# A transformer step's mixture-of-experts stage: one chunk body, w1/w3 as the moving operand in three fp32r products, chunks in expert order, rows scattered to tokens

## The reference

```python
def _hier_moe(x, w_group, b_group, w_expert, b_expert, w1, w3, w2):
    xt = x.reshape(b * t, d)                                   # 640 x 1024
    g_p, g_idx = lax.top_k(softmax(xt @ w_group + b_group), 1)
    e_sel = ...                                                # the 4 logits of the chosen group
    e_p, e_idx = lax.top_k(softmax(e_sel), 2)
    gate_w = g_p * e_p / sum(e_p)
    combine = sum(one_hot(g_idx * 4 + e_idx, 16) * gate_w[..., None], axis=1)
    hidden = silu(xt @ w1[e]) * (xt @ w3[e])                   # w1, w3: 1024 x 256, for each e
    return sum_e (hidden * combine[:, e]) @ w2[e]              # w2: 256 x 1024

def _block(x, mod, mixer, ln, moe):
    sh1, sc1, g1, sh2, sc2, g2 = jnp.split(mod[:, None, :], 6, axis=-1)
    y, extras = mixer(x * (1.0 + sc1) + sh1)
    x = _layer_norm(DEEPNORM_ALPHA * x + g1 * y, ln[0], ln[1])
    return _layer_norm(DEEPNORM_ALPHA * x + g2 * _hier_moe(x * (1.0 + sc2) + sh2, *moe), ln[2], ln[3])
```

## Time and profile before

| | |
|---|---|
| median of three runs | 1844.82 us |
| the profiled execution, its own time | 1840.76 us |
| its span, first to last instruction | 1839.0 us |
| mean granted TensorE clock | 0.911 |
| TensorE matmul busy | 1471.5 us, 80% of the span |
| TensorE weight load busy | 1123.9 us, 61% |
| VectorE busy | 737.2 us, 40% |
| ScalarE busy | 425.1 us, 23% |
| GpSimd busy | 220.7 us, 12% |
| moved by DMA | 277.62 MB, mean 151 GB/s |

### The profile page before, as it was taken

How to read it: one execution, slowest core, us unless ns; L and a number is a source line. 1 busy time by engine, 2 the same in 40 slices (tenths; PEclk the granted TensorE clock), 3 DMA queues, 4 the chain that set the end, 5 groups by cost and what they waited for, 6 DMA issues and landing times. The chain is left out here.

```text
span 1839.0 us, 22558 instructions
## 1 busy us (share of the span) xinstructions
PE 1471.5 (80%) x8207; PEld 1123.9 (61%) x8208; DVE 737.2 (40%) x1363; ACT 425.1 (23%) x832; POOL 220.7 (12%) x170
## 2 busy tenths in 40 slices
PE   3699999546888997589993199989997857999970
PEld 1577777446565444578882188877874436777760
DVE  0321212076477343211114835439993750111118
ACT  0321212143343111011112312225551111101113
POOL 1100000022000032100003500010000321100016
PEclk9899999769899998699997599999998877999995
DMA  7665555700000901559994032110007126777763
GB/s 256 227 221 199 199 200 193 174 12 15 17 1 2 298 35 61 176 175 357 358 351 157 35 111 75 58 49 1 1 1 231 57 92 233 273 269 250 258 219 143
DMA packets 177697, 277.62 MB, mean 151 GB/s; under 512 B 13400, under 2 KB 111408, under 8 KB 177616
## 3 DMA queue, kind: packets, MB, share of 16 engines
q1 hardware_dynamic: 167232, 239.15, 38.7%
q0 software_dynamic: 9520, 34.24, 5.3%
q10 hardware_dynamic: 864, 3.15, 0.4%
HBM read 246.90 MB, written 34.85 MB: 153 GB/s over the span
## 5 line engine op out<-in xcount | busy, mean ns | idle before, releaser
L485 PE MATMUL psum<-in_parts 128*128 128x460 f32 (+2 forms) x1800 | 400.1, 381 | 23.2 <-PEq L336 23.2
L485 PEld LDWEIGHTS psum<-in_parts 128*128 128x128 f32 x1800 | 337.2, 189 | 101.6 <-issue 53.0
L785 PE MATMUL psum<-layer 128*128 128x512 f32 x400 | 174.2, 595 | 2.7 <-PEq L711 2.7
L1919 PEld LDWEIGHTS psum<-layer 128*128 128x128 f32 x1280 | 145.7, 192 | 15.1 <-issue 7.7
L1919 PE MATMUL psum<-layer 128*128 128x128 f32 x1280 | 146.4, 275 | 6.7 <-DVE layer L2124 6.7
L1919 PEld LDWEIGHTS psum<-layer,arena 128*128 128x128 f32 x1152 | 135.3, 197 | 13.5 <-issue 7.1
L1919 PE MATMUL psum<-layer,arena 128*128 128x128 f32 x1152 | 136.1, 280 | 5.6 <-DVE layer L2124 3.6
L785 PEld LDWEIGHTS psum<-layer 128*128 128x128 f32 x400 | 75.9, 191 | 95.5 <-issue 95.5
L522 DVE TENSOR_TENSOR in_parts<-in,in_parts 128x920 fp32r<-128x920 f32 (+2 forms) x54 | 62.5, 1158 | 167.3 <-ACT in_parts L517 167.3
L2114 DVE TENSOR_TENSOR layer<-psum,layer 128x256 f32<-128x256 f32 x32 | 13.6, 424 | 222.7 <-ACT layer L2084 222.7
L517 ACT CAST in_parts<-in 128x920 fp32r<-128x920 f32 (+2 forms) x54 | 53.7, 994 | 165.1 <-PE psum L485 154.1
(11 more groups left out here) (312 smaller groups left out, 1980.1 us busy)
## 6 DMA issues: line engine op xcount, KB each, us to landing
arena<-in_moe_w SPq DMA_DIRECT2D x48, 1024.0 KB, 9.3
layer<-in_moe_w SPq DMA_DIRECT2D x48, 1024.0 KB, 8.8
in<-in_ada_w SPq DMA_DIRECT2D x40, 1024.0 KB, 5.7
y_rows<-layer SPq DMA_DIRECT2D x64, 256.0 KB, 8.7
in<-in_od_w_in SPq DMA_DIRECT2D x21, 512.0 KB, 3.6
in<-in_ev_w_in SPq DMA_DIRECT2D x21, 460.0 KB, 3.6
start<-in_ada_w SPq DMA_DIRECT2D x8, 1024.0 KB, 16.2
arena<-mod_rows SPq DMA_DIRECT2D x16, 512.0 KB, 8.6
```

Of the source, the lines that this page charges most:

```text
L485: last = T.matmul(bank(g % W_BANKS)[:, 0:cw], a, b[:, kk], start=(k == 0 and m == 0), stop=(k == KD - 1 and m == 2))
L785: last = T.matmul(bank(g % 4), feats[k][:, t * P:(t + 1) * P], wout[:, k, j * BANK:(j + 1) * BANK], start=(k == 0), stop=(k == kt - 1))
L1919: last = T.matmul(dst[:, (2 * f + m) * P:(2 * f + m + 1) * P], weights[m][:, k, f * P:(f + 1) * P], xT[:, k, :], start=(k == 0), stop=(k = ...
```

## The change

- `up` has the operands the other way round. The turned tokens (128 tokens, 128 features) are the stationary operand, and 128 columns of w1 beside 128 of w3 are the moving one, 256 columns. Both are split in two fp32r parts, high and low, and three products are made (x high by w high, x high by w low, x low by w high): 2 halves of the hidden width x 8 feature blocks x 3 = 48 matmuls of 256 columns. The result has tokens on partitions, so the hidden values must be turned (2 transposes and 2 copies) before `down`, which stays.
- ScalarE makes the high parts (a copy to fp32r), VectorE the low parts (a difference): of the weights, 4 pieces of 128x1024 per expert and engine; of the tokens, 2 pieces of 128x512 per chunk and engine. Expert 0's high parts are made in `router`.
- Chunks are numbered in expert order. All use one body; an expert's last chunk also splits the next expert's weights. The second body is gone. The number of chunks is the same.
- Padded rows carry an index out of bounds, and the gather and the store leave them out. What a chunk puts out is scattered by GpSimd to the row of its (choice, token) in `y_rows`, which now has 1280 rows.
- `xg` and `yb` are single buffers. GpSimd's loop per chunk q: wait for the turn of chunk q+1, gather chunk q+2, wait for the copy-out of chunk q, scatter it, wait until it has landed, and release `yb`.
- The weight loads are in rows of 4 KB throughout (w1 and w3 in halves of 512 KB each). SyncE issues w1 and w3 of expert e+2 when expert e's parts are made, and w2 when its last `down` is done. The loads for `combine` come at the end.
- `combine` loads `y_rows` in five plain transfers of 1 MB on SyncE's queue. The zeros and their waits are gone. The router has three VectorE instructions fewer in the middle and four more behind the last product.

The core of the diff:

```diff
-                        sp.dma_start(y_rows[NE * P:, :], zero_row.partition_broadcast(FURTHER * P)
-                                     ).then_inc(further_zero, 16)
...
-                        sp.wait_ge(further_zero, 16)
...
+        def up_high_of(act, b, f, h):
+            return A.copy(part_up(0, f)[:, h * HK:(h + 1) * HK], raw_piece(b, f, h))
+
+        def up_low_of(dve, b, f, h):
+            ks = slice(h * HK, (h + 1) * HK)
+            return V.tensor_tensor(part_up(1, f)[:, ks], raw_piece(b, f, h), whole(part_up(0, f)[:, ks]), ALU.subtract)
...
+                    def refill(p, b):
+                        e = 2 * p + b
...
+                        for h in range(2):
+                            sp.wait_ge(up_low, read[h])          # read = 4 * e + 3 + h
+                            load_up(sp, b, h, ups[h])            # w1, w3 of e + 2
+                        sp.wait_ge(y_s, done)
+                        load_down(sp, b, dn)                     # w2 of e + 2
...
+                    def gather(q):
+                        pool.indirect_dma_start(out=xg, out_offset=None, in_=h2_rows, in_offset=column(from_i, q, 0),
+                                                bounds_check=TOK - 1, oob_is_err=False).then_inc(xg_in, 16)
+
+                    def scatter(q):
+                        pool.wait_ge(y_a, q + 2)
+                        pool.indirect_dma_start(out=y_rows, out_offset=column(to_i, q, 1), in_=yb.rearrange("p j n -> p (j n)"), in_offset=None,
+                                                bounds_check=2 * TOK - 1, oob_is_err=False).then_inc(y_out, 16)
+                        pool.wait_ge(y_out, 16 * q + 16)
+                        pool.nop().then_inc(y_free, 1)
+
+                    gather(0)
+                    last = entry(pool, 2, LAST)
+                    pool.wait_ge(turned, 1)
+                    gather(1)
+                    with pool.Fori(0, last) as q:
+                        pool.wait_ge(turned, q + 2)
+                        gather(q + 2)
+                        scatter(q)
+                    scatter(last)
...
+                    def up(q, e, f):
+                        for h in range(2):
+                            pe.wait_ge(x_high, 2 * q + 1 + h)
+                            pe.wait_ge(up_low, 4 * e + 2 * f + h + 1)
+                            for k in range(h * HK, (h + 1) * HK):
+                                for n in range(2):
+                                    T.matmul(UP[f][:, 0:2 * P], x_h[:, k, :], part_up(n, f)[:, k], start=(k == 0 and n == 0), stop=False)
+                        for h in range(2):
+                            pe.wait_ge(x_low, 2 * q + 1 + h)
+                            for k in range(h * HK, (h + 1) * HK):
+                                last = T.matmul(UP[f][:, 0:2 * P], x_l[:, k, :], part_up(0, f)[:, k], start=False, stop=(k == KD - 1))
+                        last.then_inc(up_used, 1)
...
+                    def chunk(q, p, b, more):                    # TensorE
+                        for f in range(2):
+                            up(q, 2 * p + b, f)
+                        turn_hid(q, 0)
+                        turn_x(q + 1)
+                        turn_hid(q, 1)
+                        down(q, p, b, 0)
+                        down(q, p, b, 1).then_inc(y_s, 1)
...
+                    def put(q):                                  # ScalarE
+                        act.wait_ge(y_s, q + 1)
+                        act.wait_ge(y_free, q + 1)
+                        A.copy(yb, bank(5, 2).rearrange("p (j n) -> p j n", j=2)).then_inc(y_a, 1)
+
+                    def chunk(q, p, b, more):
+                        silu(q, 0)
+                        if more:
+                            high_up(p, b, 0)
+                        silu(q, 1)
+                        copy_hid(q, 0)
+                        high_x(q + 1, 0)
+                        copy_hid(q, 1)
+                        high_x(q + 1, 1)
+                        if more:
+                            high_up(p, b, 1)
+                        put(q)
...
+                    for t in range(NT):
+                        sp.dma_start(yg[:, t], y_of[t]).then_inc(y_in[t], 16)
```

More of the change, by code:

```diff
@@ L1941, in entry @@
             def entry(eng, row, e):
                 col = tables[0:1, row, e:e + 1] if isinstance(e, int) else tables[0:1, row, bass.ds(e, 1)]
-                return eng.value_load(col, min_val=0, max_val=(NT - 1) if row == 0 else FURTHER + 1)
-            def further(eng, e, chunk):
-                n = entry(eng, 0, e)
-                first = entry(eng, 1, e)
-                with eng.If(n > 0):
-                    with eng.Fori(0, n) as c:
-                        chunk(nc.s_assert_within(first + c, 0, FURTHER - 1, skip_runtime_bounds_check_because=(
-                            "two experts for each token fill at most FURTHER chunks beyond the first ones")), c)
-                eng.nop()
+                lo, hi = ((0, NT - 1), (0, CHUNKS - 2), (0, CHUNKS - 2))[row]
@@ new lines, in entry, with segments, segment @@
+                return eng.value_load(col, min_val=lo, max_val=hi)
+            def segments(eng, chunk):
+                def segment(p, b, more):
+                    e = 2 * p + b
+                    n, first = entry(eng, 0, e), entry(eng, 1, e)
+                    with eng.If(n > 0):
+                        with eng.Fori(0, n) as c:
+                            chunk(nc.s_assert_within(first + c, 0, CHUNKS - 2, skip_runtime_bounds_check_because=(
+                                "two experts for each token fill at most CHUNKS - 2 chunks")), p, b, False)
+                    eng.nop()
+                    chunk(entry(eng, 2, e), p, b, more)
+                with eng.Fori(0, NE // 2 - 1) as p:
+                    segment(p, 0, True)
+                    segment(p, 1, True)
+                segment(NE // 2 - 1, 0, True)
+                segment(NE // 2 - 1, 1, False)
@@ L2019, in _ @@
-                    gather(0, 0)
-                    loop(pool, expert)
-                    pool.wait_ge(o_out, entry(pool, 2, NE - 1) * 16)
+                        return bass.IndirectOffsetOnAxis(ap=rows[:, n:n + 1], axis=0)
+                    def gather(q):
[7 more added lines that the diff above has]
+                        pool.nop().then_inc(y_free, 1)
@@ L2104, in _ @@
+                    segments(act, chunk)
                 @block.vector
                 def _(dve):
[L2106 to L2130 removed]
@@ L2134, in _ @@
+                    for h in range(2):
+                        low_up(0, 0, 0, h)
+                    for h in range(2):
+                        low_x(0, h)
+                    for h in range(2):
+                        low_up(0, 0, 1, h)
+                    segments(dve, chunk)
                     dve.drain()
```

382 lines of the change are left out of this document (160 added, 222 removed).

## The result

The changed kernel takes 1892.28 us (median of four, 1889.49 to 1896.09), the kernel before 1845.26 on the same chip: a ratio of 1.0252, with a 95% interval of 1.0225 to 1.0279. Slower was the likelier side, and the time lies in the range; but the loss is 47 us where 23 were forecast. Between the profiled executions (1893.6 against 1840.76) it is 52.8 us. The mean granted TensorE clock fell from 0.911 to 0.889.

What follows compares the result with a forecast made beforehand. TensorE was taken to bound the kernel before, with the DMA engines at their limit too. GpSimd's chain +34, seams -7, -5 and +4 gave +26 on 1840.76, 1867, given as 1868 us; range 1833 to 1917, with nearer rivals 1795 to 1925.

Steps and rivals of the forecast that it cites:

- GpSimd's chain: Expert stages: gather, scatter and wait for its landing in series on GpSimd's queue; 14.2 us per chunk with loads, +34 in all.
- Lg: GpSimd's queue: the landing time of a chunk's gather, 4.2 us quiet, 7.7 with loads over it.
- P: GpSimd's period per chunk, both landings plus 2.3 us: 10.7 quiet, 14.2 with loads over one transfer.
- full landings: Gathers and scatters priced as if padded rows still cost their time: 4.2 us quiet, 7.7 loaded.
- Rival 2: TensorE's `up`: 256-column matmuls stay at 0.215 us, body 15.3 in all 38 chunks; +100, 1940 us; chance 0.10.
- rival 1: Expert stages: landings do not pile up, TensorE stays the bound; 1820 us, or 1778 with shorter landings; chance 0.30.
- ScalarE and VectorE "at nothing": Expert chunks: 7.6 and 7.1 us of work beside TensorE's 11.0, costed at nothing; would show if the body were under 8.
- The seams: Stretches around the expert stages and before layer 0's mixer: three terms of -7, -5 and +4 us.
- (a): Before layer 0's mixer: `mod_rows` no longer stands behind 5 MB of zeros; -7 us (0 to -8).
- (b): Start of each expert stage: first gather no longer waits behind 2 MB of `combine` loads; -5 us in all (+2 to -7).
- (c): End of each expert stage, last `down` to combine's first work: 13.0 us for 11.1; +4 in all (-4 to +10).
- Rival 4: Gathers and scatters: leaving out rows may cost descriptors all the same; changes nothing in the sum; no chance given.

Runs made afterwards that it cites:

- e2: Changed kernel with a semaphore wait for the drain behind the column's copy, and the scatter-landing wait moved behind the next gather's issue: 1789.54 us, ratio 0.972.
- e1: Changed kernel with GpSimd's drain behind the column's copy replaced by a wait for that copy's own semaphore: 1870.69 us, ratio 1.016.
- e5: Changed kernel, drain kept, with only the wait for a scatter's landing moved behind the next gather's issue: 1869.26 us.
- e4: Changed kernel with the weight loads of experts 2 to 15 cut to five DMAs of 32 KB each, all waits kept: 1780.07 us.
- e10: Kernel before with only the w1 and w3 loads changed to the changed kernel's layout, packets of 4 KB for 1 KB: 1842.89 us beside 1844.12.
- e3: Changed kernel with w1 and w3 loaded in the kernel before's layout, rows of 1 KB for 4 KB: 1861.57 us, ratio 1.010.
- e8: Changed kernel with padded rows moved after all, gathered from the last token's row and scattered to one spare row: 1913.19 us.
- e9: Changed kernel with each expert's w1 and w3 loads held until the gather in flight has landed: 1898.19 us.
- e7: Changed kernel with the drain replaced by a semaphore, the scatter-landing wait moved, and 1 KB load rows: 1770.47 us, ratio 0.961.
- e11: Changed kernel with 12 of the 48 matmuls of `up` left out in each chunk: 1886.53 us.
- e12: e7 with 12 of the 48 matmuls of `up` left out in each chunk: 1762.12 us beside e7's 1770.47.

## Why the prediction came out as it did

**Right in sign and mechanism.** The term that decides is the one named: GpSimd's two landings in series (103 us for taking both links away in e2, 22 and 23 for one of them in e1 and e5), with TensorE idle ahead of the token transposes. e4 shows that without loads there is no loss at all.

**The step that failed** is in "GpSimd's chain", where Lg was taken from the earlier trace rows: "That one takes 7.7: P = 7.7 + 4.2 + 2.3 = 14.2". By parts:

- The quiet half came out, by luck: scatter to the next gather 5.6 priced (4.2 + 1.4), 5.6 measured in the rows above. But the scatter at 904.62 lands in 3.2, not 4.2, and what follows it takes 2.4, not 1.4, 0.8 of it because the copy of the column takes 0.97 where 0.18 was priced.
- The loaded half didn't: gather to scatter 8.5 priced (7.7 + 0.8), 10.0 measured. 7.7 was a landing beside rows of 1 KB. The change makes them 4 KB, and the prediction used that only to shorten the burst ("perhaps 8 with longer rows", an estimate; beside a loaded gather the loads move at 0.26 MB per us with rows of 1 KB and at 0.27 with 4 KB). The same gather of 128 rows is through at 7.8 beside rows of 1 KB and at 8.9 beside rows of 4 KB (the kernel before and e10, means with over 2 MB of loads). e3 takes the length back in the changed kernel and gets 1861.6, 6 us under the forecast of 1868, with a mean period of 14.3 over the 28 chunks. That it comes so near is luck in part: the forecast took full landings, and e3 leaves the padded rows out, which was worth 21 us in the changed kernel (e8). So the rows' length, 31 us, is the larger part of the 45 by which the forecast missed with full landings (an estimate, as e3 and e8 were not run together); what is left of the 45 stays open.
- "Over one of the two transfers of each period" is true of about every second chunk only. In the others the loads touch both, 7.4 + 7.6, for nearly the same sum; e9, where the scatter takes nearly all of it, has 15.6. The simplification cost next to nothing.
- 28 chunks x 1.2 = 34 us. The stages came to 540 where 511 were forecast, 29 over. The difference is in the ten other chunks and the start, 109 where 113 were priced: quiet chunks took 9 to 11 in place of 11.0.

**TensorE's terms** held. `up` was priced at 6.0; its 48 matmuls run from 1000.83 to 1007.14 at a granted clock of 1.00, 6.3 with the gaps:

```profile
1000.83 2.47 PE L2031 MATMUL psum<-moe_parts 128*128 128x256 f32 x16
...
1003.14 1.12 PE L2035 MATMUL psum<-moe_parts 128*128 128x256 f32 x8
...
1004.10 2.08 PE L2031 MATMUL psum<-moe_parts 128*128 128x256 f32 x16
...
1006.02 1.12 PE L2035 MATMUL psum<-moe_parts 128*128 128x256 f32 x8
```

No run shows the 0.125 us for one matmul behind the 6.0, nor the 5.6 that bounds it from below; these 48 make it 0.131, gaps included. Nor does any run show a level of 1.2 GHz, by which the forecast prices 3 us for the first `up` of each stage. The views give the clock as a share of full speed: it is 0.50 from 754.53 to 758.00 and from 1555.01 to 1561.00, and the first `up` of the two stages takes 8.6 and 8.0 us where 6.3 is the time at 1.00, 4.0 more in all. In the kernel before it is 0.50 from 762.41 to 765.00, and the two take 8.92 and 9.95 where 7.31 is the time at 1.00.

The body of 11.0 is what e4 and e7 measure. The granted clock fell to 0.89 and 0.90 in the two stages, from 0.99 and 0.98, and cost little: a quarter fewer matmuls in `up` gave 6 us (e11). Rival 2 (0.215 a matmul) is out, as is rival 1: the landings do pile up.

**ScalarE and VectorE "at nothing"** was right for this kernel and wrong in its reason. I compared sums (7.6 and 7.1 against 11.0) and wrote that they would show below 8; e12 shows them, with the scatter's landing that ScalarE waits for among them, just under 11. 16 table loads of 1.28, with 18 us of stall ahead of them, were not in the sum at all. They are eight in each stage.

**The seams** gave 11.8 where 8 were forecast.

```profile
351.34 0.81 SPq L626 DMA_DIRECT2D mod_rows<-in  x2
...
353.84 0.37 SPq L924 DMA_DIRECT2D layer<-in_ret_decay_fwd  x1
```

(a) From `mod_rows` to the mixer 2.5 us in place of 11.3: 8.8 for the 7 forecast. At the expert stage 4.6 are left: 1.0 was lost ahead of it and some 3 in the mixer, where TensorE's granted clock from 457.4 to 496.9 us was 0.85, and 0.92 over the same work before (465.7 to 503.4). (b) The first gathers: -9.1 for -5; the one of layer 0 lands without the 2 MB beside it (last packet 4.0 us after its issue at 746.80, 7.8 after that at 751.31 before). (c) The end: +0.1 for +4, as the last scatter, of 86 rows, was landed and the next loads issued 3.55 us after its issue, where 5.5 were priced (4.2 + 1.3):

```profile
1011.73 1.01 ACT L2091 COPY moe<-psum 128x1024 f32<-128x1024 f32 x1 [2.30 <-PE psum L2049]
...
1014.02 0.99 POOL L1998 DMA_INDIRECT y_rows<-moe  x1 [0.93 <-issue]
1017.57 2.75 SPq L2161 DMA_DIRECT2D arena<-y_rows  x5
1023.00 1.15 ACT L2182 ACTIVATE arena<-arena 128x1024 f32<-128x1024 f32 x1 [10.26 <-DMA arena<-y_rows]
```

**Rival 4** (left-out rows cost descriptors all the same) is half true: as many packets, but 21 us saved (e8).

Open: why the first packet of a transfer behind a burst moves only 4.5 to 5.2 us after its issue (means), where it is 1.6 to 1.9 with nothing beside it. It is the same with rows of 1 KB (e3) as of 4 KB, so the length of the loads' rows doesn't explain it. The gathers of the kernel before have it too (4.6 with over 2 MB beside them), so the 7.7 had it in it.

## What to carry to other kernels

A landing time read from a trace belongs to the packets that run beside it (gathers of 128 rows were through at 7.8 us on the mean beside rows of 1 KB, and at 8.9 beside rows of 4 KB): when an edit changes the layout of the loads, take the landing again, beside packets of the new size. Before you price a chain with two transfers on one queue, ask what makes it a chain; here a wait and a drain each did so, and only both together were worth removing (103 us, where each alone gave 22). And an engine whose busy sum is two thirds of the period can still be next in line when, in its queue, small work that TensorE waits for stands behind long casts or behind a wait for a landing (e12: 39.9 us of TensorE's waits).

## What the runs showed of the hardware that I had not expected

- A drain on GpSimd stood until the indirect transfer issued ahead of it had landed, gather or scatter, with no instruction that waits for it: 2.5 us at 871.63 in e5, up to 9.8 in the changed kernel. There each of the 36 scatters that follow a gather goes out 1.2 to 1.9 us behind the gather's last packet, and in e5 no indirect transfer goes out sooner than 1.15 behind the last packet of the one ahead. With a semaphore on the copy in place of the drain (e1) the idle time is 0.5 us, and the scatter at 885.16 goes out 2.1 us behind the gather's issue.
- Loads in packets of 4 KB in place of 1 KB stretched a gather beside them by 1.4 us, from first to last packet, at nearly the same rate of the loads (0.27 and 0.26 MB per us in the changed kernel and e3; 2.5 to 3.9 us from e3 to the changed kernel, 3.2 to 4.6 from the kernel before to e10).
- Rows that the bounds leave out shortened a gather by 0.8 us when nothing ran beside it (last packet at 3.2 against 4.1), and not at all when over 2 MB of loads did (8.6 us to its last packet with 66 rows of 128 on the mean, and with all 128 in e8).
- GpSimd's copy of one column takes 0.18 to 0.20 us in 64 of 78 cases in the changed kernel. The other 14 were issued while one of VectorE's differences of 128x1024 was under way, take 0.6 to 1.1 us, and each ends 0.04 us behind that difference (0.97 at 908.40).
